# Convolution taps in pairs on four 64x64 quarters of TensorE, and the sum of squares of its norm one step sooner

## The reference

```
def causal_depthwise_conv(x, w, b):
    """x: (B,S,C), w: (K,C), b: (C,). y_t = sum_k w_k x_{t-K+1+k} + b."""      # K = 31, C = 512

def even_mixer(h, w_in, w_out, dw_w, dw_b, ln_g, ln_b):
    proj = h @ w_in
    q, k, v, u, gate = jnp.split(proj, [...])
    a_out = merge_heads(stick_breaking_attention(q, k, v heads))               # 8 heads of 64
    c = u * jax.nn.sigmoid(gate)
    c = causal_depthwise_conv(c, dw_w, dw_b)
    c = jax.nn.silu(layer_norm(c, ln_g, ln_b))
    return jnp.concatenate([a_out, c], axis=-1) @ w_out
```

## Time and profile before

| | us |
|---|---|
| median of three runs | 1450.81 (1449.68 to 1451.09) |
| profiled execution | 1449.5 |
| its span, first to last instruction | 1447.7 |
| TensorE busy | 1418.4 |
| VectorE, ScalarE, GpSimd busy | 945.8, 720.4, 165.5 |

### The profile page before, as it was taken

One profiled execution on the slowest core, in us unless ns is written; L12 is line 12 of the kernel. 1 busy time (PEld: TensorE's weight loads), 2 busy tenths in 40 slices (PEclk: granted clock), 3 DMA queues, 4 the chain that ended last, 5 costly groups with the idle time before them and its releaser, 6 DMA issues.

```text
span 1447.7 us, 17857 instructions
## 1 busy us (share of the span) xinstructions
PE 1418.4 (98%) x6695; PEld 1170.0 (81%) x6695; DVE 945.8 (65%) x1321; ACT 720.4 (50%) x1054; POOL 165.5 (11%) x262
## 2 busy tenths in 40 slices
PE   7999999999999999999999999999999999999997
PEld 5888888778888888888888888887877788788886
DVE  5666667777665677665786776665468566655543
ACT  5454455565444455543754544445555634544442
POOL 1900010010000010000162100001542110100000
PEclk9999999999999999999999999999999999999999
DMA  8685755246876778768533588674845355465551
GB/s 282 201 256 202 261 198 202 66 145 191 247 231 214 251 233 260 244 216 263 204 121 124 169 222 264 229 238 144 216 161 204 118 175 174 160 204 175 182 207 62
DMA packets 236341, 286.50 MB, mean 198 GB/s; under 512 B 37028, under 2 KB 160464, under 8 KB 236256
## 3 DMA queue, kind: packets, MB, share of 16 engines
q1 hardware_dynamic: 236000, 285.25, 61.1%
q10 hardware_dynamic: 256, 0.11, 0.0%
HBM read 281.13 MB, written 4.20 MB: 197 GB/s over the span
## 4 chain that ended last, share of the span: by engine, by line
PE 91%; ACT 3%; DVE 3%; DMA 2%; issue 2%; POOL 0%; ACTq 0%; DVEq 0%; POOLq 0%
PE ps L571 28%; PE ps L574 27%; PE ps L572 27%; PE ps L857 2%; DMA raw<-in_w_in_dram 1%; PE ps L1108 1%; PE ps L743 1%; ACT whi L460 1%; DVE wlo L469 1%; PE ps L1391 1%; PE ps L1059 0%; ACT junk L683 0%; PE ps L996 0%; ACT xh L775 0%; DMA fold<-in_norm_g_dram 0%
## 5 line engine op out<-in xcount | busy, mean ns | idle before, releaser
L469 DVE TENSOR_TENSOR wlo<-raw,whi 128x1024 fp32r<-128x1024 f32 (+2 forms) x474 | 563.1, 1222 | 243.9 <-ACT whi L460 243.5
L460 ACT ACTIVATE whi<-raw 128x1024 fp32r<-128x1024 f32 (+2 forms) x474 | 471.9, 1042 | 235.7 <-PE ps L574 95.3
L571 PE MATMUL ps<-whi,xh 128*128 128x512 f32 (+2 forms) x1440 | 567.9, 394 | 9.2 <-DVE wlo L469 6.7
L572 PE MATMUL ps<-wlo,xh 128*128 128x512 f32 (+2 forms) x1440 | 555.4, 386 | 0.0
L574 PE MATMUL ps<-whi,xl 128*128 128x512 f32 (+2 forms) x1440 | 548.3, 386 | 0.0
L571 PEld LDWEIGHTS ps<-whi,xh 128*128 128x128 f32 x1440 | 271.0, 188 | 67.8 <-DVE wlo L469 9.3
L574 PEld LDWEIGHTS ps<-whi,xl 128*128 128x128 f32 x1440 | 270.7, 188 | 55.6
L572 PEld LDWEIGHTS ps<-wlo,xh 128*128 128x128 f32 x1440 | 271.2, 188 | 50.7
L571 PE MATMUL ps<-whi,gh 128*128 128x512 f32 x440 | 172.6, 392 | 0.0
L572 PE MATMUL ps<-wlo,gh 128*128 128x512 f32 x440 | 171.3, 389 | 0.0
L574 PE MATMUL ps<-whi,gl 128*128 128x512 f32 x440 | 153.5, 389 | 0.0
(11 more groups left out here) (239 smaller groups left out, 915.7 us busy)
## 6 DMA issues: line engine op xcount, KB each, us to landing
raw<-in_ffn_w_in_dram SPq DMA_DIRECT2D x174, 512.0 KB, 5.4
raw<-in_ffn_w_out_dram SPq DMA_DIRECT2D x40, 1024.0 KB, 5.7
raw<-in_w_in_dram SPq DMA_DIRECT2D x26, 1024.0 KB, 4.9
adat<-in_w_ada_dram SPq DMA_DIRECT2D x96, 256.0 KB, 2.9
raw<-in_w_ffn_gate_dram SPq DMA_DIRECT2D x22, 512.0 KB, 3.9
raw<-in_w_ffn_up_dram SPq DMA_DIRECT2D x22, 512.0 KB, 4.9
raw<-in_hyb_w_in_dram SPq DMA_DIRECT2D x10, 1024.0 KB, 5.5
raw<-in_gla_w_in_dram SPq DMA_DIRECT2D x10, 1024.0 KB, 5.1
```

What stands on the lines that cost most here:

```text
L460: e.activation(split_of(whi, j), raw_of(j), ACT.Copy).then_inc(*whi_made.up(j))
L469: e.tensor_tensor(split_of(wlo, j), raw_of(j), split_of(whi, j).bitcast(F32), ALU.subtract).then_inc(*wlo_made.up(j))
L571: e.matmul(ps[:, 0:n], a, whi_of(j, k), start=first and k == 0, stop=False)
L572: last = e.matmul(ps[:, 0:n], a, wlo_of(j, k), start=False, stop=False)
```

## The change

Four things change in the mixer of stage 1.

1. A tap on TensorE is two matmuls of 64x64 (upper and lower half of the channels) in place of one of 128x128. For a tap with an even place in the list, the halves stay where they are: rows 0 to 63 give output partitions 0 to 63, rows 64 to 127 give 64 to 127, and the sum goes to the tile "conv". For an odd place the halves are exchanged: rows 0 to 63 give outputs 64 to 127 and the reverse, into a second tile, "convx". At the end ScalarE copies "convx" to SBUF, and two 64x64 matmuls with the identity, 512 columns each, add it to "conv" with the halves exchanged back (`pe_taps_join`).
2. TensorE has 42 taps (block 2 from k = 20 on), VectorE 82. GpSimd makes 42 diagonals of 128x64, after one addition that folds the identity to that form.
3. Blocks of taps are 10, 8, 6, 6, 6 and 6 taps, where they were 8 and five times 6. In VectorE's queue 20 taps stand before the third pair's logarithms, where 26 stood, and the first value comes behind them, where it came ahead; later 11 taps stand where 8 stood. In ScalarE's queue the copy of "convx" stands ahead of the third value, and taking out block 3 waits for the join.
4. The sum of squares stands in TensorE's queue ahead of step 2, where it stood ahead of step 3, and so do its parts on ScalarE and VectorE.

```diff
-            diag = sb("diag", 38 * P, where=inner)
+            diag = sb("diag", 43 * 64, where=inner)
...
-        NT = 24
+        NT = 20
         PE_TAPS = [(2, k) for k in range(NT, 31)] + [(3, k) for k in range(31)]
         TAPS = [(b, k) for k in range(31) for b in range(3) if b < 2 or k < NT]
...
                 if i == 0:
-                    tb.next(("conv",), (taps_joined,), (conv_out,))
-                    for done in tb.freed:
-                        e.wait_ge(*done)
+                    for name, last in ((("conv",), [(taps_joined,), (conv_out,)]), (("convx",), [(convx_made,)])):
+                        tb.next(name, *last)
+                        for done in tb.freed:
+                            e.wait_ge(*done)
                     e.wait_ge(*diag_made.at(len(PE_TAPS) - 1))
                     e.wait_ge(*cx_made.at("u", 2))
-                t = e.matmul(tb.of("conv")[:, (b - 2) * 256:(b - 1) * 256], diag[:, i * P:(i + 1) * P], cx_of(b, k),
-                             start=i == 0, stop=k == 30, skip_group_check=True)
+                ps = tb.of("convx" if i % 2 else "conv")
+                for p in (slice(0, 64), slice(64, P)):
+                    q = slice(64 - p.start, P - p.start) if i % 2 else p
+                    t = e.matmul(ps[q, (b - 2) * 256:(b - 1) * 256], diag[p, i * 64:(i + 1) * 64], cx_of(b, k)[p, :],
+                                 start=i < 2, stop=i % 2 == 1 and k >= 29, skip_group_check=True)
             if (b, k) == PE_TAPS[-1]:
                 t.then_inc(*conv_dot.up())
+
+        def pe_taps_join(e):
+
+            e.wait_ge(*convx_made.at())
+            for p in (slice(0, 64), slice(64, P)):
+                q = slice(64 - p.start, P - p.start)
+                t = e.matmul(tb.of("conv")[q, :], ident[p, p], hid[1][p, 0:512], start=False, stop=True,
+                             skip_group_check=True)
+            t.then_inc(*conv_sum.up())
...
-            pe_taps(e, PE_TAPS[0:8])
+            pe_taps(e, PE_TAPS[0:10])
             pair(pe_weights, 0)
-            pe_taps(e, PE_TAPS[8:14])
+            pe_taps(e, PE_TAPS[10:18])
             pair(pe_weights, 1)
             pair(pe_values, 0)
             pe_scores(e, 2)
-            pe_taps(e, PE_TAPS[14:20])
+            pe_taps(e, PE_TAPS[18:24])
             pair(pe_values, 1)
             pe_scores(e, 3)
-            pe_taps(e, PE_TAPS[20:26])
+            pe_taps(e, PE_TAPS[24:30])
             pair(pe_weights, 2)
-            pe_taps(e, PE_TAPS[26:32])
+            pe_taps(e, PE_TAPS[30:36])
             pair(pe_weights, 3)
+            pe_taps(e, PE_TAPS[36:42])
             pair(pe_values, 2)
-            pe_taps(e, PE_TAPS[32:38])
             pair(pe_values, 3)
+            pe_taps_join(e)
...
                     pe_total(e, "mean", y_of, ...
-                if i == 3:
+                if i == 2:
                     pe_total(e, "var", sq_of, lambda b: y_square.at(b), (y_ln,))
...
+            e.wait_ge(*conv_dot.at())
+            e.activation(hid[1][:, 0:512], tb.of("convx")[:, :], ACT.Copy).then_inc(*convx_made.up())
             act_values(e, 2)
-            e.wait_ge(*conv_dot.at())
+            e.wait_ge(*conv_sum.at())
             e.activation(y_of(3), tb.of("conv")[:, 256:512], ACT.Identity, bias=vector("cb", 3)).then_inc(*conv_out.up())
             act_values(e, 3)
...
-            some(26)
+            some(20)
+            logs(2)
             dve_values(e, 0)
-            logs(2)
             some(6)
             logs(3)
             dve_values(e, 1)
-            some(8)
+            some(11)
             dve_values(e, 2)
             some(len(TAPS))
...
+            n = len(PE_TAPS)
+            two = diag[:, n * 64:(n + 1) * 64]
+            e.tensor_tensor(two, ident[:, 0:64], ident[:, 64:P], ALU.add).then_inc(*diag_made.up("two"))
+            e.wait_ge(*diag_made.at("two"))
             for i, (b, k) in enumerate(PE_TAPS):
-                e.tensor_scalar(diag[:, i * P:(i + 1) * P], ident, conv_w(b, k), None, ALU.mult
+                e.tensor_scalar(diag[:, i * 64:(i + 1) * 64], two, conv_w(b, k), None, ALU.mult
                                 ).then_inc(*diag_made.up(i))
```

More of the change, by code:

```diff
@@ L946, in program @@
         conv_dot = sig("conv_dot")
+        convx_made = sig("convx_made")
+        conv_sum = sig("conv_sum")
         conv_out = sig("conv_out")
```

## The result

| | before | changed |
|---|---|---|
| median, six runs each | 1449.78 us | 1442.20 us |
| lowest to highest | 1448.65 to 1451.09 | 1441.61 to 1443.95 |
| profiled execution, its span | 1449.5, 1447.7 | 1441.61, 1439.8 |

The ratio is 0.9948, with a 95% interval of 0.9935 to 0.9961: 7.6 us faster, forecast 7.5. The forecast was made against a median of 1450.81 of the first three runs; six runs of the kernel before give 1449.78, so 1 us of the distance between the 1443.3 forecast and the 1442.2 measured is that median's.

What follows compares the result with a forecast made beforehand. TensorE, busy 98% of the span, was taken as the bound. Gain 5.4 us to the mean, 7.75 with the late waits gone, less 0.2 given back: 7.5, so 1443.3 us from 1450.8; range 1441.3 to 1447.5.

Steps and rivals of the forecast that it cites:

- Quarters side by side, 0.432 us a pair: TensorE's taps: four 64x64 quarters work at once, so a pair of taps takes 0.432 us, half of 0.864.
- TensorE's line: TensorE's queue from first tap to down projection: 24.2 us instead of 29.84, join 1.05 included; down projection at 286.0.
- VectorE's line: VectorE's queue: 82 taps, not 86 (-1.6 us), gaps 4.8 to about 2.2; last tap at 289.35, splits done 292.4.
- The norm: Variance one step sooner, at 293.5: both waits for normalised blocks, 2.0 us, vanish.
- the step from 5.4 to 7.75: Gain up to the mean, 5.4 us, becomes 7.75 once the product at 309.84 starts at 302.1.
- Given back: Entry to the next stage: residual behind the last split and two scalings, at 308.6 not 308.4; 0.2 us lost.
- rival B: TensorE's taps: one quarter at a time or slow instruction feed; +8.6 us at 1.2 us a pair; chance 0.04.
- rival A: TensorE's taps: only two parts at a time, 0.864 us a pair; +1.3 us, 1452.1; chance 0.08.

Runs made afterwards that it cites:

- Two quarters: Changed kernel with all 42 TensorE taps on the two straight quarters, without second tile, copy or join: median 1450.84 us, ratio 1.0008.
- By quarters: Changed kernel with each block's products ordered all for one quarter, then the next, in place of tap by tap: median 1454.70 us, ratio 1.0036.
- groups of four: Changed kernel with products ordered quarter by quarter inside groups of four taps: median 1443.19 us, ratio 0.9952.
- even taps first: Changed kernel with each block's even taps first, tap by tap, then its odd taps: median 1446.48 us, ratio 0.9977.
- Variance late: Changed kernel with the sum of squares put back ahead of step 3: median 1444.50 us, ratio 0.9967.
- before, variance sooner: Kernel before with only the sum of squares moved ahead of step 2, taps as they were: median 1447.28 us, ratio 0.9981.
- logs as before: Changed kernel with VectorE's old order at the third pair (26 taps, first value, then logarithms): median 1442.26 us, ratio 0.9951.

## Why the prediction was right

**Quarters side by side, 0.432 us a pair.** Right: blocks of 2.33, 1.88 and 1.46 us from first tap to the next work, with up to 0.1 us lost ahead and 0.1 behind, where I had 2.46, 2.03 and 1.47 to 1.60 with all edges. "Two quarters" shows that with half as many at a time nothing of it is left. My reason was right in kind and loose in its limit. I wrote that the engine takes work for a free part ahead of older work for a busy one, and feared a depth of so many passes looked past. "By quarters", "groups of four" and "even taps first" show another rule: work is handed out in order, and each part has room for three waiting passes. In the change's order each quarter is handed two passes, then the next, well inside that room. The Trainium skill's rule of program order ("TensorE: Matmul & The Clock Gate", "The mechanism") does not hold across parts here: in "groups of four" the fourth quarter started ahead of nine older passes that were waiting. Within a part the passes can't be told apart in the records, so no run here tests the rule there.

**TensorE's line.** The down projection came at 286.44, forecast 286.0 with a first tap 0.19 us earlier. That is 24.46 us for 24.2 (the forecast's own terms add up to 24.3); the join took 1.01 us for 1.05.

**VectorE's line.** Waits of 0.6 and 0.9 us for the logarithms (0.4 and 0.9 forecast) and 1.05 for the third value (0.8). The join of block 2 ended at 290.0 (289.7), the centring began at 292.54 (292.4). By the forecast's own numbers the last tap would have ended at 289.2, not 289.35; it ended at 289.7.

**The norm.** Variance at 294.01 (293.5), no wait behind it. "Variance late" and "before, variance sooner" put 2.4 to 2.5 us on this edit; in the forecast it was the step from 5.4 to 7.75, 2.35.

**Given back.** Forecast 0.2 us (in rival B's +8.6, left out of rival A's +1.3), measured none. The residual started at 308.79 (308.6), and the entry of stage 2 came 7.4 us sooner (320.77 to 313.40), as did the product held at 309.84 before (now 302.55, 7.3). The shift then stayed, at 7.35 and 7.40.

**Sum.** 5.1 us for the taps and 2.5 for the norm, 7.6 in all, where I had 5.4, 2.35 and 0.2 given back. The mechanism was right, but that the sum agrees within 0.1 us is luck in part: the taps brought 0.3 us less, the norm and the term given back made up for it. The moved logarithms, which I had counted among the steps that keep TensorE from waiting, are worth nothing ("logs as before"). The four moved taps are worth 0.7 with the logarithms moved, and perhaps nothing without.

## What to carry to other kernels

A diagonal 128x128 product in fp32 can be made as two products of 64x64, on two quarters of TensorE. With the halves of every second one exchanged, all four quarters are busy, and two diagonal products take the time of one (0.43 us for 0.86 with 256 columns); each block of them loses about 0.2 us at its two edges. Order the products so that no quarter gets more than four passes in a row (six in a row already doubled the time of a block), and bring the exchanged half back on an engine with time to spare, since the join on TensorE costs 1 us. Before you price work moved between two engines, move the waits of both chains along with it: an engine that gets more work may also be released sooner, as VectorE was here with four taps more.

## What the runs showed of the hardware

TensorE hands passes to its parts in program order, and a part holds three waiting passes beside the running one: the second quarter began with the seventh pass of ten, the fifth of eight and the third of six, and in groups of four the last of four quarters began at once behind twelve older passes, nine of them waiting. From this rule the run with the even taps first was forecast: 3.65 us for its block of ten, 3.67 measured. Four of VectorE's multiply-adds of 128x256 on SBUF, in two kernels, start while GpSimd adds 128x256 in SBUF (0.73 to 1.01 us); three of them took 0.97 to 1.02 us, where 0.48 is usual; the cause was not tried by itself. GpSimd's products for the diagonals went from 600 ns (128x128) to 440 ns (128x64) in the median: half the width saves a quarter.
